# Forgetting attention's output projection: one unit of the first half moved behind the second half's first piece

## The reference, cut to what matters

```python
h_ml = ...                                   # mLSTM, 256 x 512, gated
h_fx = forgetting_attention(...)             # 256 x 512, 8 heads of 64
y = jnp.concatenate([h_ml, h_fx], axis=-1) @ w_out      # 1024 x 1024
x = layer_norm(ALPHA * x + y, ln1_g[layer], ln1_b[layer])
f = conv_ffn(x, w_up, conv_w, conv_b, w_down)           # begins with x @ w_up, 1024 x 5632
x = layer_norm(ALPHA * x + f, ln2_g[layer], ln2_b[layer])
```

## Time and profile before

| | us |
|---|---|
| median of three executions | 1211.06 |
| profiled execution, its own time | 1211.06 |
| its span (first to last instruction) | 1209.3 |
| PE busy | 1175.0 (97% of the span) |
| DVE, ACT, POOL busy | 598.1, 678.4, 939.1 |

### The profile page before, as it was taken

One profiled execution on the slowest core, in us unless ns is written; L12 is line 12 of the kernel. 1 busy time (PEld: TensorE's weight loads), 2 busy tenths in 40 slices (PEclk: granted clock), 3 DMA queues, 4 the chain that ended last, 5 costly groups with the idle time before them and its releaser, 6 DMA issues.

```text
span 1209.3 us, 19396 instructions
## 1 busy us (share of the span) xinstructions
PE 1175.0 (97%) x7328; PEld 1029.9 (85%) x7328; DVE 598.1 (49%) x1142; ACT 678.4 (56%) x944; POOL 939.1 (78%) x746
## 2 busy tenths in 40 slices
PE   6999999999989999999999999999999999999997
PEld 6888988888968998888898888888887988888885
DVE  4754354211585244221372746777405575777602
ACT  5664555353665554435446556676536665767631
POOL 6856879889933879988888545999897974999894
PEclk9999999999999999999999999999999999999999
DMA  8743545545531445554655233565564642565551
GB/s 313 225 158 124 172 143 209 193 155 187 196 105 59 152 147 211 199 174 175 217 175 174 105 140 131 200 232 205 174 209 140 220 164 72 208 219 198 203 180 35
DMA packets 33273, 208.50 MB, mean 172 GB/s; under 512 B 3448, under 2 KB 7672, under 8 KB 8744
## 3 DMA queue, kind: packets, MB, share of 16 engines
q1 hardware_dynamic: 29728, 198.17, 46.7%
q10 hardware_dynamic: 3464, 9.19, 2.3%
HBM read 206.29 MB, written 1.59 MB: 172 GB/s over the span
## 4 chain that ended last, share of the span: by engine, by line
POOL 56%; issue 21%; PE 21%; DVE 1%; POOLq 0%; DVEq 0%; ACT 0%
POOL w_lo L2741 56%; PE bank L401 6%; PE bank L297 3%; PE bank L299 3%; PE bank L298 3%; PE bank L403 3%; PE bank L358 0%; PE bank L1150 0%; PE bank L361 0%; DVE arena L2643 0%; PE bank L1180 0%; POOLq L2738 0%; PE bank L1230 0%; PE bank L1250 0%; PE bank L466 0%
## 5 line engine op out<-in xcount | busy, mean ns | idle before, releaser
L2741 POOL TENSOR_TENSOR w_lo<-raw,w_hi 128x512 fp32r<-128x512 f32 x740 | 936.4, 1305 | 252.2 <-ACT w_hi L1278 252.0
L1278 ACT ACTIVATE w_hi<-raw 128x2048 fp32r<-128x2048 f32 x185 | 352.3, 1911 | 159.8 <-DMA raw<-stream 72.0
L401 PE MATMUL bank<-xs,w_hi 128*128 128x512 f32 x960 | 339.4, 399 | 0.0
L403 PE MATMUL bank<-xs,w_lo 128*128 128x256 f32 x960 | 269.6, 281 | 0.0
L401 PEld LDWEIGHTS bank<-xs,w_hi 128*128 128x128 f32 x960 | 180.4, 188 | 44.8
L403 PEld LDWEIGHTS bank<-xs,w_lo 128*128 128x128 f32 x960 | 181.4, 189 | 0.0
L586 PE MATMUL bank<-hT,w_hi 128*128 128x512 f32 x512 | 181.0, 399 | 0.0
L297 PE MATMUL bank<-xs,w_hi 128*128 128x256 f32 x576 | 165.6, 288 | 3.5 <-POOL w_lo L2741 1.2
L298 PE MATMUL bank<-xs,w_hi 128*128 128x256 f32 x576 | 162.9, 283 | 0.0
L299 PE MATMUL bank<-xs,w_lo 128*128 128x256 f32 x576 | 162.9, 283 | 0.0
L588 PE MATMUL bank<-hT,w_lo 128*128 128x256 f32 x512 | 143.8, 281 | 0.0
(11 more groups left out here) (345 smaller groups left out, 1687.4 us busy)
## 6 DMA issues: line engine op xcount, KB each, us to landing
raw<-stream SPq DMA_DIRECT2D x185, 1024.0 KB, 4.9
arena<-ln_rows ACTq DMA_DIRECT2D x5, 1024.0 KB, 5.0
arena<-vec_scratch ACTq DMA_DIRECT2D x8, 256.0 KB, 6.3
con<-consts SPq DMA_DIRECT2D x1, 1288.0 KB
h<-x SPq DMA_DIRECT2D x2, 512.0 KB, 7.7
out<-h SPq DMA_DIRECT2D x4, 256.0 KB, 2.4
con<-pool_mat ACTq DMA_DIRECT2D x1, 768.0 KB, 6.3
vec_scratch<-vec_row ACTq DMA_DIRECT2D x1, 512.0 KB
```

Of the source, the lines that this page charges most:

```text
L401: mm(o[j][:, :], hi[:, k, s], xs[:, k, :, :].rearrange("p a t -> p (a t)"), start=(k == tiles_in[0]), stop=False, skip_group_check=True)
L403: last = mm(o[j][:, 0:T], lo[:, k, s], xs_hi[:, k, :], start=False, stop=(k == tiles_in[-1]), skip_group_check=True)
L1278: af(w_hi[:, c % CUT].rearrange("p a b -> p (a b)"), raw[:, c % RAW, :], ACT.Copy)\
L2741: ins = nc.gpsimd.tensor_tensor(w_lo[:, slot_c].rearrange("p a b -> p (a b)")[:, part], raw[:, slot_r, part], w_hi[:, slot_c].rearrange("p ...
```

## The change

A new function `last_half_held` stands in for `last_half` in this layer. Unit (0, 3) is no longer made ahead of part 1, and it no longer has a bank of its own. Its four steps (e1 on tile 1) stand behind unit (1, 0), and write the bank of (1, 3); the four steps of (1, 3) are added there later. The order of part 1 is (1, 0), the held unit, (1, 2), (1, 1), (1, 3), with no interleaving. The banks of (1, 0) and (1, 1) are claimed together ahead of the first step, those of (1, 2) and (1, 3) behind (1, 0). The skip becomes five, so that part 1 keeps its banks. On VectorE `residual_half("ev_out", 3)` is gone, and the addition of (1, 3) is the one that scales `h` by ALPHA. The other layers, which have a `last_half` of their own, are not touched.

```diff
--- before.py
+++ after.py
@@ -427,6 +427,36 @@
 
                 s = slice(t * P, (t + 1) * P)
                 return three(o[:, :], src[0][:, k, s], src[1][:, k, s], hi[:, kw, :], lo[:, kw, :], start=start, stop=stop)
+
+            def last_half_held(name, i, src, wait, held):
+
+                c = START[name] + 2
+                hi, lo = half_views(c)
+                o = [claim(pe, (name, 1, t)) for t in range(TT)]
+                for k in range(4):
+                    pe.wait_ge(S("xs_ready"), XS[wait] - 3 + k)
+                    last = by_tokens(o[0], hi, lo, k, src, k, 0, start=(k == 0), stop=(k == 3))
+                filled(last, (name, 1, 0))
+                o += [claim(pe, (name, 1, 2 + t)) for t in range(TT)]
+                first_hi, first_lo = half_views(START[name] + 1)
+                for k in range(4):
+                    last = by_tokens(o[3], first_hi, first_lo, k, held, k, 1, start=(k == 0), stop=False)
+                used_up(last)
+                hi2, lo2 = half_views(c + 1)
+                for k in range(4):
+                    last = by_tokens(o[2], hi2, lo2, k, src, k, 0, start=(k == 0), stop=(k == 3))
+                filled(last, (name, 1, 2))
+                for k in range(4):
+                    last = by_tokens(o[1], hi, lo, k, src, k, 1, start=(k == 0), stop=(k == 3))
+                used_up(last)
+                filled_by_chunk((name, 1, 1), c)
+                for k in range(4):
+                    last = by_tokens(o[3], hi2, lo2, k, src, k, 1, start=False, stop=(k == 3))
+                    if k == 2:
+                        first_turned(i, 0)
+                used_up(last)
+                filled_by_chunk((name, 1, 3), c + 1)
+                first_turned(i, 1)
 
             def last_half(name, i, src, wait, sums=lambda: None):
 
@@ -1131,10 +1161,8 @@
                     evacuated(pe, "m_rows")
                     rotating[0] = 8
                 fox_step(p)
-            half_piece("ev_out", 0, 6, (xm_hi, xm_lo))
-            half_piece("ev_out", 0, 7, (xm_hi, xm_lo))
-            turn[0] += 4
-            last_half("ev_out", 5, (xf_hi, xf_lo), "fx")
+            turn[0] += 5
+            last_half_held("ev_out", 5, (xf_hi, xf_lo), "fx", (xm_hi, xm_lo))
             beside_by_tile("fup0", 5)
             keep_gate_banks("fup0")
             dense_beside("fup0", 22, first=2)
@@ -1943,7 +1971,7 @@
                     dst = hh if to_h else z
                     if factor is not None:
                         ins = v.scalar_tensor_tensor(dst, z, factor[:, t:t + 1], hh, ALU.mult, ALU.add)
-                    elif i == 5:
+                    elif i == 5 and (n, t) != (1, 1):
                         ins = v.tensor_tensor(dst, z, hh, ALU.add)
                     else:
                         ins = v.scalar_tensor_tensor(dst, hh, ALPHA, z, ALU.mult, ALU.add)
@@ -2605,8 +2633,7 @@
                     residual_half("ev_out", 0)
                     residual_half("ev_out", 1)
             residual_half("ev_out", 2)
-            residual_half("ev_out", 3)
-            for n in range(4):
+            for n in range(3):
                 evacuated(dve, ("ev_out", 0, n))
             norm(5)
             gated("fup0", 0)
```

## The result

The changed kernel takes 1215.55 us (median of 14 executions) and the kernel before 1211.79 us in the same measurement: 3.76 us more, a ratio of 1.0038 with a 95% interval from 1.0027 to 1.0050. It is slower, by 0.3 to 0.5%. The ratio goes with the means rather than with the medians. Of the fourteen executions one took 1934.75 us, at a mean granted clock of 0.557 (the ratio leaves it out), and four took 1217.5 to 1221.5 us, of which there is no profile. The forecast was 1212.9 with a range up to 1214.6, which the result lies above. The profiled execution took 1215.61 us, its span 1213.8.

What follows compares the result with a forecast made beforehand. The prediction took TensorE, busy 97% of the span, as the bound. It added only the new wait's 1.85 us, all other terms nothing, to 1211.06, giving 1212.9 us, with a range of 1210.9 to 1214.6.

Steps and rivals of the forecast that it cites:

- The pause: TensorE ahead of part 1: waits for VectorE's addition of (0, 2) to free the bank of (1, 1), losing 1.85 us.
- The clock: TensorE behind the new pause: granted clock stays 1.00, as behind the 1.90 us pause at 368.53, so no cost.
- rival D: Part 1 on TensorE: the clock falls, 60 matmuls at twice the spacing add 13.6 us, giving 1226.5; chance 0.02.
- The lead of tile 0: Handover to the normalization: tile 0's results, 1.4 us earlier relative to the end of (1, 3), gain 0.
- all that a better order could win here: Handover on TensorE: three pauses of 1.19, 0.41 and 0.45 us, ended by VectorE's low parts, together 2.05 us.
- The chunk e1: Its slot is freed later behind the held unit, delaying the next chunk's load; cost nothing, 1.6 to 2.8 us of cover.
- Rival C: ScalarE and GpSimd: the late chunk decides; if GpSimd took twice its 5.02 us, 1215.1, slower; chance 0.07.
- A: Handover: tile 0's lead shortens the pauses by up to 1.4 us, giving 1211.5, or 1210.9 without pauses; chance 0.10.
- B: Ahead of part 1: no new wait, so the 1.85 us is missing; at best 1209.0; chance 0.05.
- VectorE's first addition of the normalization: VectorE in `norm(5)`, once (1, 0) is filled: named as a sign, expected at about 721.2.
- The removed addition: VectorE: one addition of 0.69 us goes, but VectorE had nothing to do until (1, 0) was filled; gain nothing.
- the sum in one bank: TensorE: the held unit adding into the bank of (1, 3) costs nothing.

Runs made afterwards that it cites:

- e1: Changed kernel with the bank of (1, 1) claimed behind unit (1, 0), not ahead of it; against the kernel before, median +0.02 us, ratio 1.0003.
- e3: Changed kernel with VectorE adding unit (0, 2) ahead of pair 3's low part; against the kernel before, median -0.56 us, ratio 0.9999.
- g3: g2_lead_used with tile 1's transposes behind the products of pairs 2 and 3, pair 3's low part earlier; median 1208.98 us, ratio 0.9986 to the kernel before.
- g2_lead_used: e3 with tile 0's transposes, VectorE's low parts and ScalarE's root reordered in the normalization; against the kernel before, median -0.56 us, ratio 1.0000.
- e4: Changed kernel with nine useless 512-column matmuls ahead of the early claim; against the kernel before, median +1.82 us, ratio 1.0015.
- e2: Kernel before with one added wait: TensorE waits ahead of unit (0, 3) until VectorE drained (0, 2); median +0.66 us, lowest +1.94 us, ratio 1.0009.
- f1: Kernel before with the wait of e2 and a 512-element VectorE instruction ahead of the addition of (0, 2); median +4.36 us, ratio 1.0047.
- h1: Kernel before with the wait of e2 and an 8-element VectorE instruction ahead of the addition of (0, 2); median +3.19 us, ratio 1.0029.
- f2: Changed kernel with two useless 512-column matmuls ahead of the early claim; against the kernel before, median +1.84 us, ratio 1.0013.
- h2: Changed kernel with one useless 128-column matmul ahead of the early claim; against the kernel before, median +1.45 us, ratio 1.0011.

## Why the prediction was wrong

*The pause.* Right in place, cause and releaser: TensorE stands at the claim of (1, 1)'s bank until VectorE has added (0, 2) (e1, e3). Its size was 2.01 us instead of 1.85, since the start comes 0.26 us behind the addition, outside the 0.05 to 0.15 read from the handover.

*The clock.* This step failed. The prediction took the clock's price as nothing, from the row of the pause of 1.90 us at 368 us and the window behind it, and gave rival D 0.02 at 13.6 us. What it took for a property of such a pause was one draw: in five of fourteen profiles the clock falls behind that same pause. Behind the new one it falls always or nearly so, and costs 1.54 us, since about eight matmuls run at the lower level and not all 60. With the two terms as measured, 2.01 and 1.54, the sum would have been 3.55 us, against 3.75. The rule of the Trainium skill (page "TensorE: Matmul & The Clock Gate", section "Part 1: The HAM clock gate") that an idle array goes back to the halved clock was weighed and set aside; the trace of after agrees with it, with 0.57 granted over 720 to 724. The page makes the fall depend on the array being idle for long enough, which the prediction's use of it left out. That all 60 matmuls would stay at the lower level was the prediction's own step; the spacing is back at 0.23 us from 723.93 on.

*The lead of tile 0.* Right: it was spent waiting, 1.19, 0.41 and 0.45 us before and after. Of the 2.05 us that it called "all that a better order could win here", g3 won 1.6.

*The chunk e1.* Right that it costs nothing. ScalarE began f1 at 726.71 and GpSimd ended at 728.71 + 5.03 = 733.74, 2.7 us ahead of the first L358. Rival C is out, and so are A and B, by the unchanged pauses and by the new one.

*The rest.* L1961 runs 7 times. VectorE's first addition of the normalization came at 723.87; 721.2 had been named. Of the 2.67 us between them 1.13 were there before the change, 0.16 are the longer pause, and 1.38 the lower clock: the last matmul of (1, 0) starts 1.14 us later behind the restart (719.29 to 723.10, against 716.15 to 718.82 for the same twelve) and takes 0.24 longer. The removed addition and the sum in one bank show no effect: e1 and e3 have both and stand at the time of before.

## What to carry to other kernels

When the order of work is changed, follow each claim of a buffer to the instruction that frees it, and put the claim directly ahead of its first use; a claim taken in a list with others makes work wait that needs none of them. Price a new pause of TensorE twice, as its length and as what the clock may do behind it, and look for similar pauses in several executions before taking one row as an answer. A lead on one engine's work gains nothing until the lists of the engines that use it are moved as well.

## What had not been expected of the hardware

A pause of 1.94 to 2.33 us between dense matmuls was followed by about 3 us at the 1.2 GHz level, which began 0.7 to 1.3 us after the restart and cost 1.5 to 1.6 us each time; pauses of 1.12 to 1.74 us at the same place were not. With the same instruction order, a pause of 1.90 to 1.92 us at 368 us did it in five profiles of fourteen, so one profile says little about such a pause. Nor is 3 us the most that it costs: in g2_lead_used the clock was at 0.50 from 58 to 64 us, behind a pause of 2.41 us:

```profile
57.99 1.98 PE L827 MATMUL bank<-arena 128*64 128x256 f32 x8 [2.41 <-ACT arena L1382]
...
58.00:61.00 3.00, 3.00 (x14) 1.76 (x16) 1.22 (x2) 1.92 (x2) 1.63 (x3) 0.50 1.13 223
61.00:64.00 3.00, 3.00 (x16) 2.35 (x13) 1.92 (x4) 0.60 (x3) 3.00 (x3) 0.50 1.11 279
```

Useless matmuls put into such a pause paid for themselves: e4 has the late start and is 1.9 us faster in the median than the changed kernel, each against the kernel before of its measurement. And the time from the end of VectorE's addition to TensorE's restart was 0.05 to 0.06 us in e2, f1 and h1, 0.11 in f2 and h2 with their useless matmuls ahead of the pause, and 0.26 in the changed kernel; why was not tried.
